# First norm on a third of the modulation, the rest of it made inside the RWKV rounds, and low-rank products on h and the difference

## The chip, the cores and the metric

The kernel runs on one core of one Trainium2 chip. The metric is the device time of one launch in microseconds: 3759.18 us is the median of three runs of the kernel before (3757.04 to 3760.25). TensorE (PE), VectorE (DVE), ScalarE (ACT), GpSimd (POOL) and SyncE (SP) run their own instruction streams, written out by hand, and hand over through semaphores. All DMAs are issued by SP, in program order.

## What is computed

The reference is a block of two layers (RWKV-7 time mix with MLP, then forgetting attention with MLP) and a second block (gated delta net, latent attention, mixture of experts), on 512 tokens of width 1024 in float32. The change touches only the first layer's modulation and time mix:

```python
c_act = silu(c)
mod = c_act @ mod_w[0] + mod_b[0]                 # 1024 -> 6144
sh1, sc1, gt1, sh2, sc2, gt2 = split(mod, 6)
h = rms_norm(x, norm_mix_g[0]) * (1 + sc1) + sh1
xx = token_shift(h) - h
xr, xw, xk, xv, xa, xg = (h + xx * mu[j] for j in range(6))
r, k, v = xr @ wr, xk @ wk, xv @ wv
w_log = -softplus(-(w0 + tanh(xw @ w1) @ w2)) - 0.5      # w1: 1024x64
a = sigmoid(a0 + (xa @ a1) @ a2)                          # a1: 1024x64
g = sigmoid(xg @ g1) @ g2                                 # g1: 1024x160
y = wkv7_scan(r, exp(-exp(w_log)), k, v, ...)             # in chunks of 64 tokens
x = x + (1 + gt1) * ((group_norm(y) + bonus) * g) @ wo
x = x + (1 + gt2) * mlp(rms_norm(x) * (1 + sc2) + sh2)
```

## The kernel before

Activations lie as 128 channels by 512 tokens in eight tiles (`x3`, `h3`). Weights pass through `W`, a ring of five slots of 128 x 2048 floats (1 MB). `load` takes the next slot, waits on SP until its former content is free (on DVE for kinds that begin with "md", on PE otherwise), and issues the DMAs. Because SP is one queue, a load that waits for its slot holds back every later one.

**Modulation.** The row of 6144 numbers is made in 12 groups of 512 columns, each from two 1 MB tiles. Of seven groups (0, 2, 4, 6, 7, 9, 11) DVE makes the sum over eight column blocks: one multiplication (L73) and seven multiply-adds (L76), accumulated in `rowb`; then four products of PE with a column of ones put the 512 sums into four columns of bank 6. The five groups in `MOD0_PE` are made by PE itself, with the activation of c as weights, and turned into columns in the same way over `rowp`. The function `dv_mod` waits for the last group, adds the bias and writes `mod0`, 48 columns: 0 to 7 shift, 8 to 15 scale, 16 to 23 gate, 24 to 47 those of the MLP. Only then does `dv_norm` form the gain and multiply x by the inverse root; ACT (`ac_normed`) scales and shifts tile by tile into `h3`.

**Mixing.** `dv_mix` makes the eight differences `xx3`. Then it forms the mixed inputs of w, a and g one tile at a time into two buffers in `MX`, each of which waits until PE has used the one two before; `pe_lora` multiplies each by w1, a1 or g1 (g1 in two parts of 96 and 64 columns, four banks in all). DVE then makes the mixed inputs of k and r, GpSimd (`gp_mix`) that of v. Before these loads `sp_mix` parks X in DRAM, since X is scratch in the rounds. The second low-rank weights (`lw2`) lie in slot 4 for the whole of the rounds, so the ring has four slots there.

**Rounds.** The 1024 channels are done in eight column blocks. Each passes five stages: `fetch` (k, r, v: 24 products of 128x128 by 512), `prep` (decay, normalised key), `scores` (chunk matrices and their inverse in five levels), `chain` (the state over eight chunks), `post` (group norm, gate, bonus). Round r runs chain on block r-3, scores on r-2, post on r-4, prep on r-1 and fetch on r. `woven` advances the stages by one step each in that order (3, 2, 4, 1, 0), on each engine by itself; a `yield` ends a step, and a stage has some 24 steps. So the position of an instruction in its engine's queue is set by its step and its stage, and a wait holds all that follows it on that engine. SP loads for round r two slots ("rk" with k and r, "rv" with v), and from round 4 a small one ("rg") with the gate's weights for `post`. After round 11, PE projects with `rw_wo` and DVE adds the result, scaled by one plus the gate, to the restored X.

Of the kernel before, what the change touches and what calls it, by code (L numbers as in the profile page):

```python
# [10 lines left out]
P = 128  # L11
T = 512
D = 1024
KT = 8
# [196 lines left out]
def program(nc, a, out):  # L211

    ctx = ExitStack()
    with ctx:
# [331 lines left out]

        cv = Carve()
# [5 lines left out]
        MX = cv(1024)  # L553
        omka = mods[:, 176:184]

        def sp_mix(sp):
            sp.wait_ge(s_ac, nac["nm", "mix0", 7])
            sp.dma(xpark, X[:, :]).then_inc(s_park, 16)
            load(sp, ("l1",), (0, (0, P), (8, 64), rows128(a["rw_w1"])), (512, (0, P), (8, 64), rows128(a["rw_a1"])),
                 (1024, (0, P), (8, 96), rows128(a["rw_g1"][:, 0:96])))  # L560
            load(sp, ("l2",), (0, (0, P), (8, 64), rows128(a["rw_g1"][:, 96:160])))
            ring.turn = NS - 1
            load(sp, ("lw2",), (0, (0, 64), (1024,), a["rw_w2"]), (0, (64, 128), (1024,), a["rw_a2"]),
                 (1024, (0, P), (640,), a["const"][:, NCON:NCON + 640]))
            ring.slots = NS - 1

        def dv_mix(dv):
            for k in range(KT):
                dv.wait_ge(s_ac, nac["nm", "mix0", k])
                dv.tt(xx3[:, k, 1:T], h3[:, k, 0:T - 1], h3[:, k, 1:T], SUB).then_inc(s_dv, ndv())  # L570
                dv.ts(xx3[:, k, 0:1], h3[:, k, 0:1], -1.0, None, MUL, None).then_inc(s_dv, ndv("xx", k))

            def mix(o, j, k):
                dv.wait_ge(s_dv, ndv["xx", k])
                return dv.stt(o, xx3[:, k, :], col("rw_mu", 8 * j + k), h3[:, k, :], MUL, ADD)

            n = 0
            for j in (1, 4, 5):
# [5 lines left out]
            for d, j in ((1, 2), (0, 0)):  # L584
                for k in range(KT):
                    mix(xm[d][:, k, :], j, k).then_inc(s_dv, ndv("xm", d, k))
            for k in range(KT):
                dv.wait_ge(s_gp, ngp["xm", k])
            dv.ts(omka, col("rw_ka", 0, 8), -1.0, 1.0, MUL, ADD).then_inc(s_dv, ndv("mixed"))

        def gp_mix(gp):
            for k in range(KT):
                gp.wait_ge(s_dv, ndv["xx", k])
                gp.ts(xm[2][:, k, :], xx3[:, k, :], col("rw_mu", 24 + k), None, MUL, None).then_inc(s_gp, ngp())
                gp.wait_ge(s_gp, ngp.n)
                gp.tt(xm[2][:, k, :], xm[2][:, k, :], h3[:, k, :], ADD).then_inc(s_gp, ngp("xm", k))

        def pe_lora(pe):
            k1, t1_ = ring["l1",]
            k2, t2_ = ring["l2",]  # L600
            w1v, a1v, g1v = [wv(k1, o, (0, P), (8, w)) for o, w in ((0, 64), (512, 64), (1024, 96))]
            g1w = wv(k2, 0, (0, P), (8, 64))
            n = 0
            for j in (1, 4, 5):
                for k in range(KT):
                    mb = MX[:, (n % 2) * 512:(n % 2) * 512 + 512]
                    f, l = k == 0, k == KT - 1
                    pe.wait_ge(ring.sems[k1], t1_)
                    pe.wait_ge(s_dv, ndv["mx", n])
                    if j == 1:  # L610
                        m = pe.mm(BK[0][0:64, :], w1v[:, k, :], mb, f, l)
                    elif j == 4:
                        m = pe.mm(BK[1][64:128, :], a1v[:, k, :], mb, f, l)
                    else:
                        pe.mm(BK[2][0:96, :], g1v[:, k, :], mb, f, l)
                        pe.wait_ge(ring.sems[k2], t2_)
                        m = pe.mm(BK[3][0:64, :], g1w[:, k, :], mb, f, l)
                    if n == 23:
                        npe.mark_next("free", "l1")
                        npe.mark_next("free", "l2")  # L620
                    m.then_inc(s_pe, npe("lora", n))
                    n += 1

        def ac_lora(ac):
            ac.wait_ge(s_pe, npe["lora", 7])
            ac.act(LO[0:64, :], BK[0][0:64, :], ACT.Tanh).then_inc(s_ac, nac("lo", 0))
            ac.wait_ge(s_pe, npe["lora", 15])
            ac.act(LO[64:128, :], BK[1][64:128, :], COPY).then_inc(s_ac, nac("lo", 1))
            ac.wait_ge(s_pe, npe["lora", 23])
            ac.act(ZG[0:96, 0:512], BK[2][0:96, :], ACT.Sigmoid).then_inc(s_ac, nac("lo", 2))  # L630
            ac.act(ZG[0:64, 512:1024], BK[3][0:64, :], ACT.Sigmoid).then_inc(s_ac, nac("lo", 3))
# [19 lines left out]
        XS, UU = cv(64), cv(64)  # L651
        yg = h3
# [30 lines left out]
        def pe_fetch(pe, ct, left):  # L683

            yield from idle(2)
            for j, name in enumerate(("k", "r", "v")):
# [6 lines left out]
                for k in range(KT):  # L693
                    if j == 2:
                        pe.wait_ge(s_gp, ngp["xm", k])
                    else:
                        pe.wait_ge(s_dv, ndv["xm", (1, 0)[j], k])
# [6 lines left out]
                    if k % 4 == 3:  # L704
                        yield from idle(3)

# [300 lines left out]
        def pe_chain(pe, ct):  # L1007
# [79 lines left out]
        def sp_post(sp, ct):  # L1087
            cs = slice(ct * 128, ct * 128 + 128)
            load(sp, ("rg", ct), (0, (0, 96), (128,), a["rw_g2"][0:96, cs]), (128, (0, 64), (128,), a["rw_g2"][96:160, cs]))

        def pe_post(pe, ct, left):
# [15 lines left out]
            pe.mm(BK[2][:, :], wv(kg, 0, (0, 96), (128,)), ZG[0:96, 0:512], True, False)  # L1107
            npe.mark_next("free", "rg", ct)
            pe.mm(BK[2][:, :], wv(kg, 128, (0, 64), (128,)), ZG[0:64, 512:1024], False, True).then_inc(s_pe, npe("g", ct))
# [47 lines left out]
        def sp_rwkv(sp):  # L1157
            sp_mix(sp)
            for r in range(12):
                if r < 8:  # L1160
                    sp_fetch(sp, r)
                if r >= 4:
# [6 lines left out]
        def pe_rwkv(pe):  # L1169
            pe_lora(pe)  # L1170
            left = {0: (s_ac, nac["lo", 0]), 1: (s_ac, nac["lo", 1]), 2: (s_ac, nac["lo", 2]), 3: (s_ac, nac["lo", 3])}
# [9 lines left out]
        def gp_rwkv(gp):  # L1181
# [3 lines left out]
            gp_mix(gp)  # L1185
            rounds(none, lambda c: gp_prep(gp, c), lambda c: gp_scores(gp, c), none, none)

        def dv_rwkv(dv):
# [3 lines left out]
            rounds(none, lambda c: dv_prep(dv, c), lambda c: dv_scores(dv, c), lambda c: dv_chain(dv, c), lambda c: dv_post(dv, c))  # L1192
# [1867 lines left out]
        def tensor_program(pe):  # L3060
            pe_start(pe)
            pe_squares(pe, "mix0", 7)
            run(pe_mod(pe, "mod0", 6144, 0, 6, MOD0_PE))
# [10 lines left out]
        def scalar_program(ac):  # L3074
# [5 lines left out]
            ac_mod(ac, "mod0", MOD0_PE)  # L3080
# [8 lines left out]
        def vector_program(dv):  # L3089
            dv_start(dv)  # L3090
            run(dv_mod(dv, "mod0", mod0, 6144, 0, col("mod_b0", 0, 48), 6, MOD0_PE))
# [112 lines left out]
```

## Time and profile before

| | |
|---|---|
| median of three runs | 3759.18 us (3757.04 to 3760.25) |
| the profiled execution | 3766.57 us, span 3764.8 us |
| mean granted clock of PE | 0.962 |
| busy, share of the span: PE / DVE / ACT / POOL | 94% / 38% / 19% / 11% |
| DMA | 452.62 MB, mean 120 GB/s |

A row of the timeline gives the start and the length of a merged group of instructions, the engine, the line, the operation, what it writes and reads, the count, and in brackets how long the engine stood idle before it and what ended that. Most matrix products of this kernel are recorded under line 79, a helper's, and most vector operations under L70, L73 and L76; they are told apart by tiles, shapes and order. In float32 one product of the program is two MATMUL instructions in the trace.

### The profile page before, as it was taken

The page shows a single profiled execution, that of the slowest core. Times are in us where ns is not written, and L with a number is a line of the kernel's source. Part 1 is how long each engine was busy: PE and PEld are TensorE (multiplying, and loading weights), DVE is VectorE, ACT ScalarE, POOL GpSimd, SP SyncE. Part 2 cuts the span into 40 slices and gives each one's busy share as a digit, 9 for nine tenths or more (in the row PEclk, how much of TensorE's full clock was granted, in tenths as well). Part 3 has the DMA queues.
Part 4 walks back from the last instruction along what each step waited for, and adds up shares of the span by engine and source line. Part 5 has one row for each costly group of instructions (what it writes and reads, how often), then busy time and mean ns, then how long its engine had stood idle before and what let it go on. Part 6 is the DMA issues. An engine that isn't in the chain of part 4 may idle for free.

```text
span 3764.8 us, 54477 instructions
## 1 busy us (share of the span) xinstructions
PE 3527.6 (94%) x24282; PEld 2173.7 (58%) x24282; DVE 1419.7 (38%) x2543; ACT 733.5 (19%) x1480; POOL 398.9 (11%) x310
## 2 busy tenths in 40 slices
PE   6699999899999999999998999998979999899998
PEld 2256667488884547588885566665434444434343
DVE  4543444288753005388633445453012211211011
ACT  1132333211003014211003222332012210200001
POOL 1210110123002000123001110102000001200000
PEclk8899998899999899999998999997989999999999
DMA  8310001255551120156522111000021114399996
GB/s 302 89 41 26 25 12 36 90 157 177 181 179 57 45 90 12 45 157 192 165 72 65 46 35 28 31 24 2 34 73 33 34 45 158 140 406 409 409 409 279
DMA packets 352746, 452.62 MB, mean 120 GB/s; under 512 B 18624, under 2 KB 258496, under 8 KB 352256
## 3 DMA queue, kind: packets, MB, share of 16 engines
q1 hardware_dynamic: 352512, 449.13, 34.8%
q8 instruction: 191, 3.13, 0.3%
q14 instruction: 43, 0.35, 0.0%
HBM read 444.87 MB, written 4.19 MB: 119 GB/s over the span
## 4 chain that ended last, share of the span: by engine, by line
PE 87%; DVE 5%; ACT 4%; DMA 2%; issue 1%; SPq 0%; POOL 0%; POOLq 0%; DVEq 0%; ACTq 0%
PE bank L79 87%; ACT A L87 2%; DVE A L76 1%; DVE A L70 1%; DMA A<-in_w_up 1%; ACT SM L87 1%; ACT H L87 0%; DMA W<-in_w_up 0%; ACT A L86 0%; DVE H L70 0%; SPq L93 0%; DVE X L76 0%; PE bank L82 0%; POOL SM L70 0%; DVE A L73 0%
## 5 line engine op out<-in xcount | busy, mean ns | idle before, releaser
L79 PE MATMUL bank<-A 64*64 64x64 f32 (+7 forms) x13408 | 1031.3, 261 | 62.2 <-ACT A L87 41.8
L79 PEld LDWEIGHTS bank<-A 64*64 64x64 f32 (+3 forms) x13408 | 813.6, 149 | 296.7 <-issue 134.6
L79 PE MATMUL bank<-A,W 128*128 128x512 f32 (+3 forms) x2336 | 829.6, 509 | 37.2 <-DMA W<-in_rw_g 18.4
L79 PE MATMUL bank<-H,W 128*128 128x512 f32 (+1 forms) x1776 | 694.5, 546 | 23.6 <-ACT H L87 11.4
L79 PEld LDWEIGHTS bank<-A,W 128*128 128x128 f32 (+2 forms) x2336 | 429.4, 189 | 383.7 <-issue 301.2
L79 PEld LDWEIGHTS bank<-H,W 128*128 128x128 f32 x1776 | 339.9, 195 | 343.0 <-issue 315.7
L87 ACT ACTIVATE A<-bank 128x512 f32<-128x512 f32 (+4 forms) x547 | 245.3, 451 | 1478.9 <-PE bank L79 1418.4
L70 DVE TENSOR_TENSOR A<-bank,A 128x256 f32<-128x256 f32 (+2 forms) x315 | 146.1, 476 | 402.3 <-PE bank L79 381.8
L79 PE MATMUL bank<-A,H 128*64 128x512 f32 (+1 forms) x1096 | 281.0, 595 | 11.7 <-ACT H L87 8.1
L70 POOL TENSOR_TENSOR A<-A 128x512 f32<-128x512 f32 (+1 forms) x111 | 155.6, 1407 | 1077.2 <-ACT A L87 372.1
L76 DVE SCALAR_TENSOR_TENSOR SM<-W,cact,SM 128x512 f32<-128x512 f32 x245 | 222.3, 907 | 11.8 <-DMA W<-in_mod_w 0.8
L79 PE MATMUL bank<-W,H 128*64 128x512 f32 (+3 forms) x952 | 212.3, 479 | 8.7 <-ACT H L87 5.5
L87 ACT ACTIVATE A<-A 128x512 f32<-128x512 f32 (+1 forms) x224 | 131.0, 609 | 448.8 <-DVE A L70 362.3
L79 PEld LDWEIGHTS bank<-A,H 128*64 128x64 f32 (+1 forms) x1096 | 89.9, 140 | 176.3 <-issue 149.5
L70 POOL TENSOR_TENSOR SM<-SM 128x512 f32<-128x512 f32 x40 | 52.3, 1307 | 1072.5 <-ACT SM L87 1070.5
L70 DVE TENSOR_TENSOR A<-bank,SM 128x512 f32<-128x512 f32 (+1 forms) x17 | 11.0, 686 | 403.2 <-PE bank L79 398.0
L76 DVE SCALAR_TENSOR_TENSOR X<-bank,mods,X 128x512 f32<-128x512 f32 (+1 forms) x120 | 81.3, 679 | 198.5 <-PE bank L79 195.1
L79 PEld LDWEIGHTS bank<-W,H 128*64 128x64 f32 (+1 forms) x952 | 87.4, 159 | 110.6 <-issue 99.9
L70 DVE TENSOR_TENSOR A<-W 128x512 f32<-128x512 f32 x128 | 91.9, 759 | 155.0 <-PE bank L79 87.5
L79 PE MATMUL bank<-A,con 128*128 128x512 f32 (+2 forms) x156 | 88.9, 658 | 20.5 <-ACT A L87 20.5
L87 ACT ACTIVATE H<-bank 128x512 f32<-128x512 f32 x56 | 31.8, 599 | 371.5 <-PE bank L79 348.1
L79 PE MATMUL bank<-H,A 128*128 128x256 f32 x384 | 93.3, 386 | 0.0
(164 smaller groups left out, 2412.5 us busy)
## 6 DMA issues: line engine op xcount, KB each, us to landing
W<-in_mod_w SPq DMA_DIRECT2D x48, 1024.0 KB, 7.2
A<-in_w_gate SPq DMA_DIRECT2D x47, 1024.0 KB, 18.5
A<-in_w_up SPq DMA_DIRECT2D x42, 1024.0 KB, 18.5
A<-in_w_down SPq DMA_DIRECT2D x40, 1024.0 KB, 18.7
W<-in_mlp_up SPq DMA_DIRECT2D x64, 512.0 KB, 5.3
W<-in_mlp_down SPq DMA_DIRECT2D x128, 256.0 KB, 3.9
W<-in_w_mod SPq DMA_DIRECT2D x24, 1024.0 KB, 5.2
W<-in_w_down SPq DMA_DIRECT2D x24, 1024.0 KB, 18.5
```

Of the source, the lines that this page charges most:

```text
L70: return self.e.tensor_tensor(o, x, y, op)
L76: return self.e.scalar_tensor_tensor(out=o, in0=x, scalar=s, in1=y, op0=op0, op1=op1, **kw)
L79: return self.e.matmul(o, l, r, start=start, stop=stop, skip_group_check=True)
L87: return self.e.activation(o, i, func, bias=bias, scale=scale)
```

## The change

Only modulation groups 0 to 3 are made before the norm: groups 0 and 2 on DVE, 1 and 3 on PE as before. Each of the other eight is made by DVE in one of rounds 0 to 7 (`dv_mod0`, stage fetch, one operation in each of steps 1, 4, 7, 10, 13, 16, 19 and 20), accumulated in `M0`, and turned into columns by PE (`pe_row0`): behind the fetch in rounds 0 to 2, ahead of the last chunk of the chain in rounds 3 to 7. Their bias is added after the rounds, in front of the gate. SP loads their two tiles in each round behind that round's k, r and v weights, through the same four slots.

The low-rank products use (h + xx mu) W = h W + xx (mu W). DVE multiplies the first low-rank weights by mu, row by row, into `LM`; PE multiplies h by the plain weights as the tiles of h appear, and then the differences by the scaled ones, into the same three banks. w1 and a1 lie side by side as one weight of 128 columns, g1 is taken as 128 and 32 columns, and the gate's second weights as 128 and 32 rows. Their loads go ahead of the parking of X and of the k, r and v weights. `gp_mix` goes, and DVE makes the mixed input of v too.

```diff
         def sp_mix(sp):
+            k, before = ring.take(("l1",), 3)
+            sp.wait_ge(...)
+            w1a1 = wv(k, 0, (0, P), (8, 128))
+            sp.dma(w1a1[:, :, 0:64], rows128(a["rw_w1"])).then_inc(ring.sems[k], 16)
+            sp.dma(w1a1[:, :, 64:128], rows128(a["rw_a1"])).then_inc(ring.sems[k], 16)
+            sp.dma(wv(k, 1024, (0, P), (8, 128)), rows128(a["rw_g1"][:, 0:128])).then_inc(ring.sems[k], 16)
+            load(sp, ("lw2",), ...)
+            load(sp, ("l2",), (0, (0, P), (8, 32), rows128(a["rw_g1"][:, 128:160])))
+            ring.slots, ring.turn = NS - 1, 1
+
+        def sp_park(sp):
             sp.wait_ge(s_ac, nac["nm", "mix0", 7])
             sp.dma(xpark, X[:, :]).then_inc(s_park, 16)
...
+            for i, (src, dst, j, c) in enumerate(((0, 0, 1, slice(0, 64)), (0, 0, 4, slice(64, 128)), (1, 1, 5, slice(0, 128)), (2, 2, 5, slice(0, 32)))):
+                n = c.stop - c.start
+                mu = col("rw_mu", 8 * j, 8).unsqueeze(2).broadcast_to([P, 8, n])
+                dv.tt(low_mu[dst][:, :, c], w[src][:, :, c], mu, MUL).then_inc(s_dv, ndv("lm", i))
+            for d, j in ((1, 2), (0, 0), (2, 3)):
                 for k in range(KT):
-                    if n >= 2:
-                        dv.wait_ge(s_pe, npe["lora", n - 2])
-                    mix(MX[:, (n % 2) * 512:(n % 2) * 512 + 512], j, k).then_inc(s_dv, ndv("mx", n))
-                    n += 1
...
+                    dv.wait_ge(s_dv, ndv["xx", k])
+                    dv.stt(xm[d][:, k, :], xx3[:, k, :], col("rw_mu", 8 * j + k), h3[:, k, :], MUL, ADD).then_inc(s_dv, ndv("xm", d, k))
...
+        def pe_lora(pe):
...
+            outs = BK[0][:, :], BK[1][:, :], BK[2][0:32, :]
+            for part in range(2):
                 for k in range(KT):
+                    if part:
+                        pe.wait_ge(s_dv, ndv["lm", 3])
                     else:
+                        pe.wait_ge(s_ac, nac["nm", "mix0", k])
+                    for o, w in zip(outs, lowrank(low_mu if part else low_loaded(), k)):
+                        m = pe.mm(o, w, (xx3 if part else h3)[:, k, :], part == 0 and k == 0, part == 1 and k == 7)
...
+        def sp_mod0(sp, r):
+            for hf in range(2):
+                load(sp, ("md", "mod0", 4 + r, hf), (0, (0, P), (4, 512), rows128(a["mod_w0"][hf * 512:(hf + 1) * 512, (4 + r) * 512:(5 + r) * 512])))
+
+        def dv_mod0(dv, r):
+            g, acc = 4 + r, M0[r % 2]
+            for hf in range(2):
+                k, there = ring["md", "mod0", g, hf]
+                v = wv(k, 0, (0, P), (4, 512))
+                for j in range(4):
+                    yield
+                    if j == 0:
+                        dv.wait_ge(ring.sems[k], there)
+                    c = cact[:, 4 * hf + j:4 * hf + j + 1]
+                    if hf == 0 and j == 0:
...
+                        m = dv.ts(acc, v[:, j, :], c, None, MUL, None)
+                    else:
+                        dv.wait_ge(s_dv, ndv["m0", r, 4 * hf + j - 1])
+                        m = dv.stt(acc, v[:, j, :], c, acc, MUL, ADD)
+                    if j == 3:
+                        ndv.mark_next("free", "md", "mod0", g, hf)
+                    m.then_inc(s_dv, ndv("m0", r, 4 * hf + j))
+                    if 4 * hf + j < 6:
+                        yield
+                        yield
...
+        def pe_row0(pe, r):
+            pe.wait_ge(s_dv, ndv["m0", r, 7])
+            for j in range(4):
+                c = 256 + 4 * r + j
+                m = pe.mm(BK[6][:, c:c + 1], M0[r % 2][:, j * 128:(j + 1) * 128], C("ones", 1), True, True)
+            m.then_inc(s_pe, npe("row0", r))
...
         # pe_fetch, at its end
+            if ct < 3:
+                pe_row0(pe, ct)
+            yield from idle(4)
...
         # pe_chain
                     pe.wait_ge(s_dv, ndv["sp", ct, c])
+                    if c == 7 and ct + 3 < 8:
+                        pe_row0(pe, ct + 3)
...
         # dv_rwkv
+            dv.wait_ge(s_pe, npe["row0", 7])
+            dv.tt(mod0[:, 16:48], BK[6][:, 256:288], col("mod_b0", 16, 32), ADD).then_inc(s_dv, ndv("mod", "mod0"))
...
-        MOD0_PE = (1, 3, 5, 8, 10)
+        MOD0_PE = (1, 3)
...
-            run(sp_mod(sp, "mod0", a["mod_w0"], 6144, MOD0_PE))
+            run(sp_mod(sp, "mod0a", a["mod_w0"], 2048, MOD0_PE))
+            sp_mix(sp)
             sp_rwkv(sp)
```

## Rows read from the trace of the kernel before

**Rows 1.** The page: chain that ended last, by engine; one DMA issue group
```profile
PE 87%; DVE 5%; ACT 4%; DMA 2%; issue 1%; SPq 0%; POOL 0%; POOLq 0%; DVEq 0%; ACTq 0%
...
W<-in_mod_w SPq DMA_DIRECT2D x48, 1024.0 KB, 7.2
```

**Rows 2.** Timeline, 0 to 110 us: modulation groups 3 and 11, one DVE group, the norm
```profile
45.38 9.88 PE L79 MATMUL bank<-W,cact 128*1 128x512 f32 x16
...
55.93 1.05 PE L79 MATMUL bank<-con,A 1*128 1x1 f32 x8 [0.68 <-ACT A L87]
...
61.16 5.54 DVE L76 SCALAR_TENSOR_TENSOR SM<-W,cact,SM 128x512 f32<-128x512 f32 x7
...
99.08 1.05 PE L79 MATMUL bank<-con,SM 128*128 128x1 f32 x8
...
101.42 5.75 ACT L87 ACTIVATE H<-H,mods 128x512 f32<-128x512 f32 x8 [3.37 <-DVE H L70]
```

**Rows 3.** SP's issues at 42 us, and low-rank weights: size, time to landing
```profile
42.29 1.47 SPq L93 DMA_DIRECT2D W<-in_mod_w  x3
...
W<-in_rw_g SPq DMA_DIRECT2D x1, 384.0 KB, 9.2
```

**Rows 4.** Timeline, 142 to 193 us: low-rank products, ScalarE behind them, first fetch
```profile
142.12 0.24 PEld L79 LDWEIGHTS bank<-A,W 128*96 128x96 f32 x2 [0.81 <-issue]
...
144.15 0.24 PEld L79 LDWEIGHTS bank<-A,W 128*96 128x96 f32 x2 [0.81 <-issue]
...
154.41 1.07 ACT L87 ACTIVATE A<-bank 96x512 f32<-96x512 f32 x2 [14.42 <-PE bank L79]
...
164.74 28.46 PE L79 MATMUL bank<-A,W 128*128 128x512 f32 x60 [10.36 <-DMA W<-in_rw_wr]
```

**Rows 5.** Stretches: busy time (and count) per engine, PE's granted clock, DMA share, GB/s
```profile
57.90:61.70 3.80, 3.80 (x6) 0.59 (x6) 1.02 (x2) 0.00 (x0) 0.00 (x0) 0.55 1.04 401
138.00:154.40 16.40, 16.38 (x33) 3.48 (x32) 8.55 (x13) 1.88 (x2) 0.00 (x0) 1.00 0.00 0
164.70:170.70 6.00, 5.96 (x7) 2.52 (x8) 0.00 (x0) 0.00 (x0) 0.00 (x0) 0.51 1.05 257
437.70:441.00 3.30, 3.30 (x38) 3.13 (x37) 0.78 (x2) 1.32 (x3) 0.00 (x0) 0.61 0.20 50
```

**Rows 6.** SP's issue that waited for the first v weights to be used
```profile
188.53 0.37 SPq L93 DMA_DIRECT2D W<-in_rw_wv  x1
```

**Rows 7.** Timeline of DVE and PE at the ends of rounds 2 and 3
```profile
260.59 0.68 DVE L70 TENSOR_TENSOR H<-bank,SM 128x512 f32<-128x512 f32 x1
...
260.73 0.33 PE L79 MATMUL bank<-A 64*64 64x64 f32 x4 [0.79 <-DVE A L1000]
...
313.96 0.68 DVE L70 TENSOR_TENSOR H<-bank,SM 128x512 f32<-128x512 f32 x1
314.56 0.27 DVE L76 SCALAR_TENSOR_TENSOR A<-A,bank 128x64 f32<-128x64 f32 x1
...
314.88 0.45 PE L79 MATMUL bank<-A 64*64 64x64 f32 x8 [0.34 <-DVE A L76]
```

**Rows 8.** PE's r product and gate product in a round; the gate weights' landing
```profile
349.47 3.70 PE L79 MATMUL bank<-A,W 128*128 128x512 f32 x8
...
355.35 2.18 PE L79 MATMUL bank<-A,W 96*128 96x512 f32 x4
...
W<-in_rw_g SPq DMA_DIRECT2D x1, 32.0 KB, 2.0
```

**Rows 9.** Timeline of PE: score products at the start of rounds 5 and 6
```profile
377.07 1.92 PE L79 MATMUL bank<-A,X 64*64 64x128 f32 x32
...
437.68 3.18 PE L79 MATMUL bank<-A,X 64*64 64x128 f32 x32
```

**Rows 10.** Middle of round 3: DVE's masked copy of a level, PE's products that read it
```profile
300.56 0.68 DVE L70 TENSOR_TENSOR A<-bank,W 128x512 f32<-128x512 f32 x1
...
303.56 3.95 PE L79 MATMUL bank<-A 64*64 64x64 f32 x128
```

More of the change, by code:

```diff
@@ L598, in pe_lora @@
[L598 to L613, printed above, removed]
-                    else:
[L615 to L622, printed above, removed]
@@ new lines, in dv_mix @@
+            for key in ("l1", "l2"):
+                k, there = ring[key,]
+                dv.wait_ge(ring.sems[k], there)
+            w = low_loaded()
+            for i, (src, dst, j, c) in enumerate(((0, 0, 1, slice(0, 64)), (0, 0, 4, slice(64, 128)), (1, 1, 5, slice(0, 128)), (2, 2, 5, slice(0, 32)))):
+                n = c.stop - c.start
+                mu = col("rw_mu", 8 * j, 8).unsqueeze(2).broadcast_to([P, 8, n])
+                dv.tt(low_mu[dst][:, :, c], w[src][:, :, c], mu, MUL).then_inc(s_dv, ndv("lm", i))
@@ new lines, in dv_mix @@
+            for d, j in ((1, 2), (0, 0), (2, 3)):
+                for k in range(KT):
+                    dv.wait_ge(s_dv, ndv["xx", k])
+                    dv.stt(xm[d][:, k, :], xx3[:, k, :], col("rw_mu", 8 * j + k), h3[:, k, :], MUL, ADD).then_inc(s_dv, ndv("xm", d, k))
+            dv.ts(omka, col("rw_ka", 0, 8), -1.0, 1.0, MUL, ADD).then_inc(s_dv, ndv("mixed"))
+        def pe_lora(pe):
+            for key in ("l1", "l2"):
+                k, there = ring[key,]
+                pe.wait_ge(ring.sems[k], there)
+            outs = BK[0][:, :], BK[1][:, :], BK[2][0:32, :]
+            for part in range(2):
+                for k in range(KT):
+                    if part:
+                        pe.wait_ge(s_dv, ndv["lm", 3])
+                    else:
+                        pe.wait_ge(s_ac, nac["nm", "mix0", k])
+                    for o, w in zip(outs, lowrank(low_mu if part else low_loaded(), k)):
+                        m = pe.mm(o, w, (xx3 if part else h3)[:, k, :], part == 0 and k == 0, part == 1 and k == 7)
+                if part:
+                    npe.mark_next("free", "l1")
+                    npe.mark_next("free", "l2")
+                m.then_inc(s_pe, npe("lora", part))
@@ new lines, in ac_lora @@
+            ac.act(ZG[:, 0:512], BK[1][:, :], ACT.Sigmoid).then_inc(s_ac, nac("lo", 2))
+            ac.act(ZG[0:32, 512:1024], BK[2][0:32, :], ACT.Sigmoid).then_inc(s_ac, nac("lo", 3))
+        def sp_mod0(sp, r):
[9 more added lines that the diff above has]
+                    if j == 0:
+                        dv.wait_ge(ring.sems[k], there)
+                    c = cact[:, 4 * hf + j:4 * hf + j + 1]
+                    if hf == 0 and j == 0:
+                        if r >= 2:
+                            dv.wait_ge(s_pe, npe["row0", r - 2])
+                        else:
+                            dv.wait_ge(s_dv, ndv["mixed"])
+                        m = dv.ts(acc, v[:, j, :], c, None, MUL, None)
+                    else:
+                        dv.wait_ge(s_dv, ndv["m0", r, 4 * hf + j - 1])
[6 more added lines that the diff above has]
+                        yield
+            yield
+            yield
+            yield
+            yield
@@ L651, in program @@
         XS, UU = cv(64), cv(64)
+        M0 = [cv(512) for _ in range(2)]
         yg = h3
@@ L3062, in tensor_program @@
             pe_squares(pe, "mix0", 7)
[L3063 removed]
+            run(pe_mod(pe, "mod0a", 2048, 0, 6, MOD0_PE))
             pe_rwkv(pe)
@@ L3079, in scalar_program @@
             ac_rstd(ac, "mix0", 7)
-            ac_mod(ac, "mod0", MOD0_PE)
+            ac_mod(ac, "mod0a", MOD0_PE)
             ac_rwkv(ac)
```

65 lines of the change are left out of this document (23 added, 42 removed).

## The prediction

> **What bounds the kernel now.** I read the page first. Its chain of the work that ended last is 87% on PE [rows 1], and PE is busy for 94% of the span, so an edit pays where PE stands still or does work that need not stand in the path. Then I read the start in order of time. The first normalised tile waits for all 24 modulation tiles. Modulation group 3 is finished on PE at 55.93 + 1.05 = 56.98 us, group 11 at 99.08 + 1.05 = 100.13 us [rows 2]; ScalarE begins the first normalised tile 1.29 us after that and needs 0.72 us for it (5.75 us for eight) [rows 2]. Everything between 56.98 and 100.13 serves columns 16 to 47 of `mod0`, which the norm does not read. After the norm comes a stretch in which the low-rank products hold PE until 154.4 us, and PE then has nothing until 164.74 us, because the projection weights stand behind them in the DMA queue [rows 4]. The first of eight fetch stages (k, r, v) gives its last weight slot back at 188.53 us [rows 6]. From there to about 640 us PE is nearly full, with short waits at the end of every round. What is added there lengthens the program; the question of this case is how much of the start's gain the rounds give back.
>
> **The change, step by step.** *Modulation.* Groups 0 to 3 keep their engines and order, so row 3 ends at 56.98 us as before: 43.15 us earlier than row 11 does now. The first tile of h is there at 56.98 + 1.29 + 0.72 = 59.0 us. The low-rank weights now follow the eighth modulation tile on SP; the slot they need is given back at 42.29 us, where the trace shows three issues in 1.47 us [rows 3]. Seven issues end by about 47 us. Their landing is bounded by that of the same weights before, 9.2 us beside the 2 MB parking transfer [rows 3]: 56 us. So they are hidden by the modulation itself, with 3 us to spare; without that cover each late microsecond would be paid in full. Parking and the first projection weights come after the last h tile (59.0 + 5.0 = 64 us), and have 45 us before anyone needs them, so the gap of 10 us before the first fetch goes.
>
> *Low-rank products.* Before, 32 products of 128x512 waited on mixed inputs; now there are 48 (three outputs, eight tiles, once on h, once on the difference), each two instructions. At half clock seven instructions took 6.0 us [rows 5], 0.857 each, so 0.43 at full clock: 96 x 0.43 = 41.2 us. They need nothing from VectorE but the eight differences (about 7 us) and four multiplications for the scaled weights (3 us, estimated by size from 0.69 us for 512 columns [rows 7]): done near 73 us, while the first half of the products alone runs to beyond 80. The 24 mixes for k, r, v are then 24 x 0.7 = 17 us on VectorE, done near 90 us, again behind PE. GpSimd's share of the mixing goes and nothing takes its place. The trace shows that four instructions alternating between 96 and 64 output columns take 144.15 − 142.12 = 2.03 us [rows 4] at granted clock 1.00 [rows 5], against 4 x 0.43 = 1.71: 0.16 us for each alternation. The new order is 128, 128, 32 columns, two alternations per tile, 32 in all: 5.1 us. Bounds: 0 (if it doesn't recur) and 0.32 each, 10 us; I take 0.16, the only row that has it.
> The Trainium skill, page "TensorEngine Tiling (Array Packing)", Key Properties, says that changing the tiling mode drains the engine. That speaks against a 32-column product between 128-column ones, and it would make 5.1 us of the 46.3; by instruction count alone the time would come out at 3727 us.
> PE restarts at 59.0 after two idle microseconds; at 57.90 us, after a similar pause, it ran for 3.8 us at granted clock 0.55 [rows 5], at the fetch for 6.0 us at 0.51. That loses half, 1.9 to 3.0 us; I take 2.5. End of the products: 59.0 + 2.5 + 41.2 + 5.1 = 107.8 us.
> ScalarE then makes tanh and a copy before bank 0 is free, two steps like the pair that took 1.07 us [rows 4], so 1.3 us with the hand-over: the first fetch starts at 109.1 instead of 164.74. It took 188.5 − 164.7 = 23.8 us, of which 3.0 were the half clock's loss [rows 5]; PE pauses for only 1.3 us now, so I drop these: end at 129.9 instead of 188.5. **Gain up to here: 58.6 us.**
>
> *Rounds.* VectorE makes one group per round, eight operations of 5.54 / 7 = 0.79 us [rows 2], 6.3 us a round, 50 us in all. In the middle of a round this is hidden: the level's masked copy is made by 301.2 us and PE reads it at 303.56 [rows 10], which leaves 2.3 us for one added operation of 0.79, and VectorE idles before the other copies. At a round's end it is not. The seventh and eighth operations stand at weave steps 19 and 20, around the state update which PE waits for. In round 3 the sequence is: output product at 313.96, ready for a successor at 314.6, state update at 314.56, PE starts 0.34 us late at 314.88 [rows 7]. With the two operations: 314.6 + 0.8, update 0.2, + 0.8 = 316.4, and then PE makes row r before it goes on. A row is 8 instructions of one column, 1.0 us (1.05 with its end [rows 2]). So 316.45 + 1.0 − 314.88 = 2.6 us for each of rounds 3 to 7: 13.0 us. In round 2 the row stands behind the last fetch: the product ends at 261.2, the operations at 262.8, the row at 263.9, where PE went on at 260.73 [rows 7]: 3.2 us. In rounds 0 and 1 VectorE is done in time, 1.0 us each. Sum 18.2 us.
> The ring now holds one round ahead instead of two. The next round's first modulation tile is issued at the end of the round and lands within 7.2 us (median of 48) [rows 1]; VectorE wants it some 4 us into the round, after its masks and the two biases, and in round 1 and 2 it will be 2 to 3 us late. There VectorE was idle for the decay anyway, and I price this at 1.0 us in all (0 to 6).
> From round 4 the gate weights go into the slot that the same round's k and r weights held. These are free at 353.2, after the r product [rows 8]; two issues of 0.4 us (three took 1.47 [rows 3]) and 2.0 us to land [rows 8] make 356.0 us, and PE wanted them at 355.35 [rows 8]: 0.7 us, in rounds 4 to 7: 2.8 us (0 to 8).
> *The clock.* After a tail of small products and waits one round, at 437.68 us, began at granted clock 0.61 [rows 5], and its first 32 score instructions took 3.18 us; after an equal tail at 377.07 they took 1.92 us [rows 9]. The balance is fine, and the tails of rounds 2 to 7 now have 2.6 us more in which PE does nearly nothing. One such start costs 3.18 − 1.92 plus 0.4 ahead of it, 1.7 us, and up to 3.0 if it lasts as at the fetch. I take 2.0 for each of the five round starts that ran at full clock: 10 us (0 to 15).
> The Trainium skill, page "TensorE: Matmul & The Clock Gate", section "HAM oscillation", warns that pauses of PE send it back to half rate; by that rule all five are paid, without it the time would be 3722 us. Which one holds this trace doesn't settle, since it has both kinds of tail.
> *Behind the rounds* VectorE adds one small addition before the gate; the first residual waits for a projection of 10 us, which hides it. The output weights are taken in other slots and land earlier; before, too, they were not waited for.
>
> **Sum.** 58.6 − 18.2 − 1.0 − 2.8 − 10 = 26.6 us. The profiled execution was 3766.57 us (span 3764.8 and 1.8 around it), which becomes 3740; it ran 7.4 us above the median of 3759.18, so on the scale of the medians I forecast **3732 us**.
>
> **Rivals.** (1) *The clock holds* and the tails overlap better: 58.6 − 14 or less, 3708 to 3718 us. For it: of the two round starts in [rows 9] one stayed at full clock, though behind a shorter tail than these will be. Chance 0.17. (2) *VectorE falls behind in the rounds*: its added 6.3 us a round does not fit between PE's hand-overs, or GpSimd's traffic stretches the 0.79 us; if each round loses 2 us more than counted, 16 us: 3748. Against it are the idle stretches before nearly every VectorE operation. Chance 0.14. (3) *The change ends slower*: the modulation tile blocks VectorE's queue at the start of each round. All masks, scans and state updates stand behind that wait, and PE behind them. It decides once a tile is later than VectorE's slack by more than 26.6 / 7 = 3.8 us in each of seven rounds; if a tile needed 7.2 us after the start of the round and each of the two tiles were waited for once, 7 x 7 = 49 us are lost, less the 1.0 counted: 3780 us. Against it: the issue comes at least 3 us before the round starts. Chance 0.05. (4) *The start gains less*: the low-rank weights land after 59 us, because their rows are short (128 to 512 bytes) and three kinds stand ahead of them, or the alternations cost 0.32; 5 to 10 us lost: 3740. Chance 0.12. The forecast itself, from 3720 to 3740: 0.52.
>
> **How the numbers follow.** The likeliest case gives 3732. The range leaves out rival 3 and the best half of rival 1: 3711 to 3750. A measurement of this kernel tells 0.2%, 7.5 us, from no change. Slower takes rival 3, 0.05; the same takes the edge of rival 2, 0.04; faster the rest, 0.91.
>
> **What would show it.** The row of group 3 ends near 57 us, PE's low-rank products start near 59 and end near 108, and the first fetch starts near 109; four instructions of 128 columns take 1.7 us and a tile's six 2.9. Each of rounds 3 to 7 should be 2.6 us longer before any change of clock, with eight one-column instructions in its tail, and its start should show a clock under 1. The gate product of rounds 4 to 7 should wait less than 1 us for its weights. I am wrong if the low-rank products wait for weights or VectorE, if the middle of a round shows new waits of PE on VectorE, or if the rounds together grow by less than 15 or by more than 50 us.

## The result, and the profile after

The changed kernel took 3726.11 us (median of six runs, 3723.16 to 3736.06) against 3759.72 for the kernel before in the same comparison; the ratio is 0.992, with a 95% interval of 0.9896 to 0.9944. I measured it twice more beside the experiments: 3727.89 against 3754.39 (ratio 0.9928, 0.9913 to 0.9943) and 3731.38 against 3756.48 (0.9929, 0.9908 to 0.9951). So the gain is 25 to 34 us, and the two later comparisons, with eleven runs of the kernel before each, say 25 to 27. The forecast was 3732 us and a gain of 26.6.

The page hardly changes, since PE bounds both (busy time of the engines and the chain; for before see the table and [rows 1]):

```profile
PE 3504.2 (94%) x24266; PEld 2169.1 (58%) x24266; DVE 1422.2 (38%) x2556; ACT 730.7 (20%) x1477; POOL 376.9 (10%) x294
...
PE 87%; DVE 5%; ACT 4%; DMA 2%; issue 1%; POOL 0%; SPq 0%; POOLq 0%; DVEq 0%; ACTq 0%
```

The start, from the timeline of the changed kernel (start, length, engine, operation, count, idle before):

```profile
54.45 1.05 PE L79 MATMUL bank<-con,A 1*128 1x1 f32 x8 [0.68 <-ACT A L87]
...
57.71 24.76 PE L79 MATMUL bank<-H,W 128*128 128x512 f32 x48 [2.21 <-ACT H L87]
...
68.82 15.98 DVE L76 SCALAR_TENSOR_TENSOR A<-A,cols,H 128x512 f32<-128x512 f32 x24
82.41 23.19 PE L79 MATMUL bank<-A 128*128 128x512 f32 x48
...
106.94 20.84 PE L79 MATMUL bank<-A,W 128*128 128x512 f32 x48 [1.34 <-issue]
```

Group 3 ends at 55.5 us, where [rows 2] had 56.98 for it; the products run without a gap from 57.71 to 105.6 us, the fetch follows after 1.34 us and ends at 127.8, where [rows 6] has 188.5. VectorE is done with its 24 mixes at 84.8 us, 22 us before anyone needs them.

The end of round 3, VectorE and PE (compare [rows 7] and [rows 9]):

```profile
260.06 0.74 DVE L76 SCALAR_TENSOR_TENSOR A<-W,cact,A 128x512 f32<-128x512 f32 x1
260.72 0.27 DVE L76 SCALAR_TENSOR_TENSOR A<-A,bank 128x64 f32<-128x64 f32 x1
260.91 0.74 DVE L76 SCALAR_TENSOR_TENSOR A<-W,cact,A 128x512 f32<-128x512 f32 x1
...
261.80 1.02 PE L79 MATMUL bank<-con,A 128*128 128x1 f32 x8 [1.75 <-DVE A L76]
...
265.08 3.00 PE L79 MATMUL bank<-A,X 64*64 64x128 f32 x32
```

The state update (260.72) stands between the two added operations, and PE waits 1.75 us for the second one before it makes the row; before, it waited 0.34 us. Then the next round starts at a lower clock: granted clock 0.62 from 265 to 268 us, and 3.00 us for the 32 score instructions instead of 1.92. In round 2, which has no chain yet, the row stands behind the last fetch:

```profile
203.62 1.05 PE L79 MATMUL bank<-con,A 128*128 128x1 f32 x8 [2.84 <-DVE A L76]
```

The lead over the kernel before, taken where the score products of a round start on PE (rounds are counted from 0, the first scores stand in round 2), shows how the rounds give the start's gain back:

| start of the scores in round | 2 | 3 | 4 | 6 | 7 | 9 | output projection |
|---|---|---|---|---|---|---|---|
| before, us | 212.01 | 260.90 | 316.83 | 437.68 | 499.18 | 600.63 | 680.15 |
| changed, us | 152.86 | 204.77 | 265.08 | 394.77 | 463.12 | 569.73 | 640.99 |
| lead, us | 59.2 | 56.1 | 51.8 | 42.9 | 36.1 | 30.9 | 39.2 |

The lead falls from 60.7 us at the first fetch's end to 30.9 where the last of the added work is behind. From there on PE runs the same instructions in both kernels (only the rows of the gate product are split otherwise, and its four instructions take 2.18 us in both), and the lead nevertheless grows to 39.2 us at the output projection and to 42.9 at the end of the span (3764.8 against 3721.9 us). The experiments show what that is.

### The profile page after: what moved, and what is told of

The parts are those of the page before. It is cut to its first block, busy times and chain, and to the rows that moved or that the text cites. A ratio compares the mean times of both kernels' runs of the same rounds, so it can differ in the third digit from the quotient of the medians.

```text
span 3721.9 us, 54427 instructions
## 1 busy us (share of the span) xinstructions
PE 3504.2 (94%) x24266; PEld 2169.1 (58%) x24266; DVE 1422.2 (38%) x2556; ACT 730.7 (20%) x1477; POOL 376.9 (10%) x294
## 4 chain that ended last, share of the span: by engine, by line
PE 87%; DVE 5%; ACT 4%; DMA 2%; issue 1%; POOL 0%; SPq 0%; POOLq 0%; DVEq 0%; ACTq 0%
PE bank L79 87%; ACT A L87 2%; DVE A L76 1%; DVE A L70 1%; DMA A<-in_w_up 1%; ACT SM L87 1%; ACT H L87 1%; DMA W<-in_w_up 0%; DVE H L70 0%; ACT A L86 0%; DVE X L76 0%; DVE SM L76 0%; POOL SM L70 0%; DVE A L73 0%; DMA A<-in_x 0%
## 5 line engine op out<-in xcount | busy, mean ns | idle before, releaser
L79 PE MATMUL bank<-A 64*64 64x64 f32 (+7 forms) x13456 | 1051.4, 261 | 62.0 <-ACT A L87 42.0
L79 PE MATMUL bank<-A,W 128*128 128x512 f32 (+2 forms) x2272 | 792.5, 504 | 9.5 <-DVE A L76 3.6
L79 PE MATMUL bank<-H,W 128*128 128x512 f32 (+3 forms) x1824 | 718.8, 548 | 26.9 <-ACT H L87 14.1
L79 PEld LDWEIGHTS bank<-A,W 128*128 128x128 f32 (+1 forms) x2272 | 420.6, 189 | 327.1 <-issue 287.4
L79 PEld LDWEIGHTS bank<-H,W 128*128 128x128 f32 (+2 forms) x1824 | 344.5, 193 | 365.1 <-issue 334.0
L87 ACT ACTIVATE A<-bank 128x512 f32<-128x512 f32 (+6 forms) x544 | 243.2, 450 | 1454.5 <-PE bank L79 1444.6
L76 DVE SCALAR_TENSOR_TENSOR SM<-W,cact,SM 128x512 f32<-128x512 f32 x210 | 193.1, 920 | 9.5
L76 DVE SCALAR_TENSOR_TENSOR X<-bank,mods,X 128x512 f32<-128x512 f32 (+1 forms) x120 | 81.2, 679 | 197.5 <-PE bank L79 194.1
## 6 DMA issues: line engine op xcount, KB each, us to landing
W<-in_w_down SPq DMA_DIRECT2D x24, 1024.0 KB, 18.4
```

What stands on the lines that cost most here:

```text
L76: return self.e.scalar_tensor_tensor(out=o, in0=x, scalar=s, in1=y, op0=op0, op1=op1, **kw)
L79: return self.e.matmul(o, l, r, start=start, stop=stop, skip_group_check=True)
L87: return self.e.activation(o, i, func, bias=bias, scale=scale)
```

## The experiments

**The reference runs.** The changed kernel, unaltered, beside the first and beside the second group of experiments.

> The changed kernel unaltered, as the reference for the runs beside it. Its trace showed the start 60.7 us ahead at the first fetch's end and 39.2 us ahead at the output projection, 42.9 us at the end of the span. Expected: 30 to 43 us faster than the kernel before. If the 3.7 us gained behind the rounds are only where PE's clock happened to fall, another execution need not show them.

> The changed kernel again, as the reference of this call. Expected within 0.3% of its other runs, 30 to 43 us faster than before.

Measured: 26.5 and 25.1 us faster than before, by the medians. From the start of the scores in round 9 to the output projection (rounds 9 to 11, the same instructions in all these kernels) the traces show 79.5 us before, 71.3 in the first profile of the changed kernel, 71.9 and 77.7 in these two; from the projection to the end 3084.7 us before and 3080.9, 3083.9 and 3084.8. So the 12 us of lead gained behind round 9 belong to the two executions that were profiled and not to the change: that of before was 10.7 us above the median of fifteen runs (3755.85), and one and the same changed kernel took 71.3 to 77.7 us for the first of the two stretches. Both expectations of 30 to 43 us were missed, 26.5 and 25.1, since they were read from that one pair of executions.

**No modulation in the rounds.** Leaves the eight later groups out.

```diff
-                    sp_mod0(sp, r)
...
-            rounds(lambda c: dv_mod0(dv, c), lambda c: dv_prep(dv, c), ...
+            rounds(none, lambda c: dv_prep(dv, c), ...
...
-            dv.tt(mod0[:, 16:48], BK[6][:, 256:288], col("mod_b0", 16, 32), ADD)
+            dv.e.tensor_copy(mod0[:, 16:48], col("mod_b0", 16, 32))
```

> Leaves out the eight later modulation groups altogether (no loads, no VectorE operations, no rows; columns 16 to 47 of the modulation are the bias alone), so it prices what the rounds pay for them. My theory (the tails pay: 1.0 us a row, 1.4 us of wait in each of five tails, 2 us in round 2, and a lower clock at six round starts): about 16 to 19 us less than the changed kernel, near 3706 us, with the middles of the rounds unaltered. Rival (VectorE is late in the middle of rounds too): more than 25 us less. Rival (the tails are hidden and only the rows cost): 8 us less.

Measured: 3694.2 us, 33.7 less than the changed kernel beside it. My 16 to 19 us were wrong, and by the number it is the rival that VectorE is late in mid-round; the trace says otherwise. From the start of the scores in round 3 to that in round 4 it takes 55.9 us against 60.5 in the changed kernel. Of that difference of 4.5, 1.76 − 0.34 + 1.02 = 2.4 stand in the tail, since the old wait of 0.34 stays; the other 2.1 are left for the lower clock around it. PE's waits for the chain's VectorE operations (L76) in the rounds are 2.0 us here and 12.0 there, where six of the seven are the waits ahead of a row:

```profile
PE bank L79 <- DVE A L76: 2.0, 6, 0.3
```

```profile
PE bank L79 <- DVE A L76: 12.0, 7, 2.8
```

(the waits from 130 to 620 us, this kernel first, then the changed one: total, times, longest). The comparison also has a flaw of mine: with fewer loads the ring ends at another slot, and the output weights are issued only at 611.07 us, when the last gate product has given its slot back:

```profile
616.57 57.39 PE L79 MATMUL bank<-H,W 128*128 128x512 f32 x128 [5.53 <-DMA W<-in_rw_wo]
```

5.53 instead of 1.42 us, so the rounds without the work are 4.1 us better than they look. From the first fetch to the projection it is 507.1 against 534.2 us; with the 4.1 the work in the rounds costs 31.2 us. The forecast of the change had 32.0 for it (rows and waits 18.2, modulation tiles 1.0, gate weights 2.8, clock 10). Where the flaw can't reach, from the first fetch to the scores of round 9, it is 432.9 against 462.3 us, 29.4 less. Of these, eight rows at full clock are 8.1, the waits for L76 10.0 less one of 0.8 us for another operation that only this kernel shows, and the gate weights 1.4; the remaining 10.7 us are left for the clock. That is the term that my 16 to 19 us left out: rows and waits alone fill them. The medians differ by more than the rounds do. In the two traces 10.7 us of the difference lie behind the start of the projection (3073.2 against 3083.9 us), where the edit changes no instruction of PE, and that part stays unexplained.

**Operations early in the round.** In pairs at steps 5, 8, 11 and 14.

```diff
-                    yield
+                    if j % 2 == 0:
+                        yield from idle(5 if hf == 0 and j == 0 else 3)
...
-                    if 4 * hf + j < 6:
-                        yield
-                        yield
-            yield
-            yield
-            yield
-            yield
+            yield from idle(10)
```

> One part altered: the eight VectorE operations of a round stand in pairs at steps 5, 8, 11 and 14, right behind the masked copy of a level, and none at steps 19 and 20; rows where they were. Tail theory: the wait of 1.76 us ahead of each row in rounds 3 to 7 falls to the old 0.34, the one of 2.84 us in round 2 to 0.8: 9 us. Clock theory: with the shorter tails the round starts return to full clock, another 5 to 10 us; so 14 to 19 us in all. If the clock falls for other reasons: 9 us and starts still at 0.6 to 0.8. If the middle of a round has no room for two operations at once, the gain is below 5 us and new waits of PE on VectorE appear there.

Measured: 3716.42 us (ratio to before 0.9898, 0.9879 to 0.9916), 11.5 less than the changed kernel beside it. Its end of round 3:

```profile
257.33 1.05 PE L79 MATMUL bank<-con,A 128*128 128x1 f32 x8 [0.34 <-DVE A L76]
...
260.26 1.92 PE L79 MATMUL bank<-A,X 64*64 64x128 f32 x32
```

The wait is the old 0.34 us, and the start runs at full clock, as do those of rounds 3, 5 and 6; rounds 7 and 8 still took 3.62 and 3.09 us. The tail theory holds: the waits for L76 are 2.0 us in total, 10.0 less than in the changed kernel, and the longest is 0.34. So the middles had room too. The clock theory holds in the trace and not in the median. From the first fetch to the scores of round 9 it takes 445.6 us instead of 462.3, 16.7 less, of which 10.0 are the waits and 6.7 are left for the clock; but the stretch from there to the projection, with the same instructions, took 77.2 instead of 71.9 (granted clock 0.86 from 560 to 620 us, 1.00 in the changed kernel). The six runs lie 18 us apart, the profiled one is the fastest, and their median falls short of the expected 14. How much of the clock part lasts to the end they don't settle.

**Fillers in the wait.**

```diff
+            for _ in range(5 if r > 2 else 8 if r == 2 else 0):
+                pe.mm(BK[6][:, 288:512], C("ones"), con[:, 0:224], True, True)
             pe.wait_ge(s_dv, ndv["m0", r, 7])
```

> PE makes extra products of constants into unused columns of bank 6 ahead of each row wait (eight in round 2, five in rounds 3 to 7, 1.9 to 3.0 us at full clock), results unused. This separates the clock from the wait: the wait stays, PE is busy in it. Clock theory: the starts of rounds 3 to 8 run at full clock, so 6 to 10 us less than the changed kernel. Rival (the clock falls whatever PE does in the tail): no gain, or 0 to 3 us slower.

Measured: 3726.26 us, 1.6 less than the changed kernel and within what the runs scatter, so the expected 6 to 10 us did not come. The trace separates what the time does not:

```profile
261.20 2.16 PE L79 MATMUL bank<-con 128*128 128x224 f32 x10 [1.00 <-DVE A L76]
...
266.02 1.92 PE L79 MATMUL bank<-A,X 64*64 64x128 f32 x32
```

With PE busy in the wait the starts of rounds 3 to 8 all took 1.92 us, where the changed kernel's took 2.7 to 3.5, and the granted clock from 200 to 560 us was 1.00 instead of 0.96. That shows that the lower clock of these six starts follows from PE's idleness in the tail. It is not all that counts: round 9, whose tail has neither a row nor fillers, now took 3.36 us, where the changed kernel's took 1.92. And the fillers can begin only after the state update, 1.00 us into the wait, and the row then starts 3.80 us after the group of 20 products ahead of it instead of 2.56: 1.2 us late in each of five rounds, 6 us in all, which eats most of what they save. From the first fetch to the projection it takes 530.3 us instead of 534.2, with two waits for gate weights (1.68 and 1.48 us) where the changed kernel had one of 1.41.

**The old products on the new order.** Modulation and loads as changed, low-rank products, their mixing and the gate's split as before.

```diff
-                        for o, w in zip(outs, lowrank(low_mu if part else low_loaded(), k)):
-                            m = pe.mm(o, w, (xx3 if part else h3)[:, k, :], ...)
+                    pe.wait_ge(s_dv, ndv["mx", n])
+                    ...
+                        m = pe.mm(BK[0][0:64, :], w1v[:, k, :], mb, f, l)
```

> Keeps the changed modulation and the early loading of the low-rank and projection weights, but makes the low-rank products as before: mixed inputs by VectorE and GpSimd, 32 products paced by two buffers. Theory A (the products' new form is what shortens the stretch from norm to fetch): fetch starts 10 us or more later than with the new form. Theory B (the new form trades a start 12 us sooner for 16 more products and their alternations, and the stretch was shortened by the loads alone): the old form takes about 49 us from the modulation's end to the fetch against 51.4, so the two kernels are within 3 us of each other. I hold B.

Measured: 3727.11 us, against 3731.38 of the changed kernel beside it and 3727.89 beside the first experiments, so no difference clear of the scatter. In the trace PE waits longer and then has less to do:

```profile
69.34 9.59 PE L79 MATMUL bank<-A,W 128*64 128x512 f32 x14 [14.28 <-DVE A L76]
```

From the addition of the bias that ends the modulation (55.10 us) to the scores of round 2 (152.46) it takes 97.4 us, with the new products 98.3 (56.53 to 154.86). Theory B holds: the algebra is worth about nothing in time.

**The narrow products together.** 128-column products of all eight tiles first, then the eight of 32 columns.

```diff
             for part in range(2):
-                for k in range(KT):
...
+                for wide in (True, False):
+                    for k in range(KT):
```

> One part altered: the eight products of 32 columns of each half are made behind the sixteen of 128 columns instead of between them: 4 alternations instead of 32. Drain theory (0.16 us for each change of width): the second half of 24 products takes 20.8 us instead of 23.2, in all 4 to 5 us less than the changed kernel. Rival (a product of 32 columns is itself slower): no change in the stretch.

Second half of the products, the changed kernel (after_same) and this one:

```profile
84.41 23.19 PE L79 MATMUL bank<-A 128*128 128x512 f32 x48
```

```profile
82.59 20.98 PE L79 MATMUL bank<-A 128*128 128x512 f32 x48
```

2.21 us for fourteen alternations fewer, 0.16 each, where the rival, a product of 32 columns that is itself slower, forecast no change: the cost goes with the changes of width. The Trainium skill, page "TensorEngine Tiling (Array Packing)", Key Properties, says that changing the tiling mode drains the engine; these two rows agree with it, though no row shows the drain itself. The fetch starts at 104.92 instead of 108.94 us. Of these 4.0 us the trace has 0.6 left at the scores of round 5 (the starts of rounds 3, 4 and 5 took 3.62 us each instead of 2.99, 2.72 and 3.30), 3.0 at those of round 9, and 0.4 at the projection (642.69 against 643.11). The other execution of the changed kernel gives 0.9, 3.0 and 6.2 at the same places. The median of 3726.53 is 4.9 us below the changed kernel beside it and 1.4 below its other reference, so the time can't tell the expected 4 to 5 us from none.

**The two halves of the change alone.** First the kernel before with only the loads of the low-rank weights put ahead of the parking:

```diff
         def sp_mix(sp):
-            sp.wait_ge(s_ac, nac["nm", "mix0", 7])
-            sp.dma(xpark, X[:, :]).then_inc(s_park, 16)
+            ring.turn = NS * 5
             load(sp, ("l1",), ...)
             load(sp, ("l2",), ...)
-            ring.turn = NS - 1
+            ring.turn = NS * 6 - 1
             load(sp, ("lw2",), ...)
-            ring.slots = NS - 1
+            ring.slots, ring.turn = NS - 1, 2
+            sp.wait_ge(s_ac, nac["nm", "mix0", 7])
+            sp.dma(xpark, X[:, :]).then_inc(s_park, 16)
```

> The kernel before with one part of the change: the low-rank weights and the second low-rank weights are loaded ahead of the parking of X, each in a slot of its own, so the projection weights no longer stand behind the last product. Modulation, products and rounds as before. By the trace of before it should save the wait of the first product (118.5 instead of about 113.4: 5 us), the gap ahead of the fetch (10.4 less 0.7: 10 us) and the half clock at the fetch's start (3 us): 18 us, 3736 to 3740 us. If instead the loads were hidden anyway, within 5 us of before.

Then the changed modulation with the old load order and the old products:

```diff
         def sp_park(sp):
             sp.wait_ge(s_ac, nac["nm", "mix0", 7])
             sp.dma(xpark, X[:, :]).then_inc(s_park, 16)
+            ring.turn = 2 * NS - 1
+            load(sp, ("l1",), ...)
+            load(sp, ("l2",), ...)
+            ring.turn = NS - 1
+            load(sp, ("lw2",), ...)
+            ring.slots = NS - 1
```

> The changed kernel's modulation (four groups ahead of the norm, eight in the rounds), with the loads behind the parking of X as before and the low-rank products as before. Start: 43 us sooner. Rounds: they pay what leaving the work out gave back, 27 to 31 us. So 12 to 16 us faster than before, 3740 to 3744 us; with the 18 us of the loads that adds up to the 27 to 30 us of the whole change. A rival is that the two halves don't add: beyond 25 us here would mean that the loads bring little by themselves.

Measured: 3742.87 us (0.9964, 0.9951 to 0.9977) and 3742.43 us (0.9962, 0.9949 to 0.9976), against 3755.85: 13.0 and 13.4 us, in sum 26.4, and the whole change measured 26.5. Each half is uncertain by about 5 us, so that the sum comes so close is luck; what holds is that neither half is the whole. The loads alone give 17.2 us of lead at the scores of round 2 (194.82 against 212.01) and 18.4 at the projection (661.78 against 680.15), as expected, though only 13.0 by the medians, which misses 3736 to 3740 us: the 18 us were read against an execution of before 10.7 us above its median, and the profiled execution here was 5.6 above its own. In the other kernel both waits of the old order are there, the second one as in [rows 4]:

```profile
74.22 7.51 PE L79 MATMUL bank<-A,W 128*64 128x512 f32 x10 [18.35 <-DMA W<-in_rw_g]
...
120.85 19.32 PE L79 MATMUL bank<-A,W 128*128 128x512 f32 x40 [10.03 <-DMA W<-in_rw_wr]
```

It has the flaw of the kernel without modulation as well: its output weights stand in another slot and are waited for 5.16 us instead of 1.42. By the difference of these two waits this half would be some 3.7 us larger without it.

**Three repairs together**, and then a fourth. The first two are the edits shown above; of the third, the buffer `G2` and its loads are shown, which SP also issues ahead of the round's other loads.

```diff
+        G2 = [cv(256) for _ in range(2)]
...
-            load(sp, ("rg", ct), ...)
+            sp.dma(g[:, 0:128], a["rw_g2"][0:128, cs]).then_inc(ring.sems[k], 16)
+            sp.dma(g[0:32, 128:256], a["rw_g2"][128:160, cs]).then_inc(ring.sems[k], 16)
```

> Three parts together: the modulation operations early in the round, the 32-column products grouped, and the gate weights in a buffer of their own, so that their loads wait for no slot of the round. By the sum of the parts (9 us of waits, 4.5 us of alternations, 1.5 to 3 us of gate weights, 5 to 10 us of clock) 20 to 26 us faster than the changed kernel, 3700 to 3706 us; without the clock part 15 us.

Measured: 3709.0 us (0.9874, 0.9851 to 0.9896), 22 us less than the changed kernel beside it and 19 less than its other reference, so above the expected 3700 to 3706 us, with a gain at the lower edge of 20 to 26. Nothing waits for gate weights any more, but the starts of rounds 4, 5, 7 and 8 were slow (3.62, 3.09, 3.62 and 2.96 us).

```diff
-                    if c == 7 and ct + 3 < 8:
+                    if c == 6 and ct + 3 < 8:
                         pe_row0(pe, ct + 3)
```

> The fastest kernel so far with one part altered: in rounds 3 to 7 the row is made ahead of the seventh chunk of the chain instead of the eighth, before the tail in which PE waits, so that the tail is 1.0 us shorter. The row itself costs PE the same. Clock theory: of four slow round starts two return to full clock, 2 to 5 us less. Rival (which tails fall into the lower clock is a matter of when they come, not of their length by a microsecond): within 2 us of it.

```profile
251.35 0.95 PE L79 MATMUL bank<-con,A 128*128 128x1 f32 x8
...
257.13 1.92 PE L79 MATMUL bank<-A,X 64*64 64x128 f32 x32
```

Measured: 3703.71 us (0.9855, 0.9836 to 0.9873), the fastest, 52 us under the kernel before. Of the round starts 3 to 9 one was slow (round 5, 3.19 us). The step from 3709.0 is 5.3 us, measured apart and with overlapping intervals, so the time alone doesn't prove it. The rows agree with the clock theory: three of the four slow starts returned, and from the first fetch to the scores of round 9 it takes 438.6 us instead of 446.6. But 4.4 of these 8.0 us are lost again on the way to the projection (78.4 against 74.0 us for the same instructions).

## Why the prediction was right, point by point

*Modulation and norm.* Right. The end of group 3 was put at 56.98 us and came at 55.5 to 56.6 in the three traces of the changed kernel, the first product at 57.7 to 58.8 instead of 59.0. The cover of the low-rank weights held: no wait for them.

*Low-rank products.* Right in size: 48.8 us forecast with half clock and alternations, 47.9 and 48.9 measured (57.71 to 105.6, 58.70 to 107.6). The 0.16 us an alternation, taken from products of 96 and 64 columns, held for 128 and 32. What the forecast had not said is that the old products would have done as well: I priced the new form without pricing the old one on the same start. The gain that was carried as one number, 58.6 us (60.7 and 58.7 measured), is the modulation and the load order alone.

*The fetch at full clock.* Right: 20.84 us, granted clock 1.00.

```profile
106.90:128.00 21.10, 21.06 (x53) 9.61 (x53) 5.75 (x8) 4.97 (x7) 0.00 (x0) 1.00 0.46 149
```

*Rows and waits.* Right. Rounds 3 to 7 were given 2.6 us each, and the trace has 1.75 − 0.34 + 1.0 = 2.4. Round 2 was given 3.2 and took 2.84 − 0.79 + 1.0 = 3.05. By the kernel without modulation in the rounds all rows and waits come to 8.1 + 10.0 − 0.8 = 17.3 us, against 18.2 in the sum.

*Loads.* Sized wrong in both terms, by little. Modulation tiles were late to VectorE twice (6.5 us in all) and at no cost to PE, where the sum had 1.0. The gate weights were forecast late by 0.7 us in each of four rounds, 2.8 in all. Three rounds show no wait of PE for them and one shows 1.48, more than the "less than 1 us" of the forecast: the smaller of the two loads (16 KB) landed 3.3 us after its issue, where the forecast had taken 2.0. Behind that wait the clock fell too, which the sum did not have:

```profile
435.93 2.19 PE L79 MATMUL bank<-A,W 128*128 128x512 f32 x4 [1.48 <-DMA W<-in_rw_g]
```

The 32 products of two 64x64 tiles that start at 438.32 us took 1.92 us, where the same ones take 1.10 in the other rounds.

*The clock.* Right in kind and size, 10 us forecast and 10.7 left for it by the kernel without modulation. The forecast took five more slow starts at 2 us. The trace has six slow starts (2.59, 3.00, 3.52, 3.00, 2.97 and 3.44 us), five more than before up to there. The other two traces of the changed kernel have six as well, in the same rounds. Rival 1, that the clock holds, fell: in the changed kernel it did not, and the fillers show why. The forecast leaned on the Trainium skill, page "TensorE: Matmul & The Clock Gate", section "HAM oscillation", for "all five are paid". The rows agree with its warning that a pause costs the clock, but the pauses that it describes are waits for DMA longer than any of these (2.84 us at most), so that these short tails are enough is shown by the runs and not by that section. Over the rounds the forecast gave back 32.0 us; the lead fell by 60.7 − 30.9 = 29.8.

*Rivals 2 and 3*, VectorE late in mid-round or blocked by a tile: no new wait of PE on VectorE in the middle of a round. *Rival 4*, a late start: no.

*The sum* stood against one execution of before, 3766.57 us, and was carried over to the median as a difference. That was needed: the pair of profiled executions differs by 42.9 us, the medians by 25 to 34. The profiled excess was put at 7.4 us from three runs, and over fifteen it is 10.7. The range, 3711 to 3750, took in no term for it. That 26.6 meets 25 to 27 so closely is partly luck: where the added work ends, the three traces have leads of 29.4 to 30.9 us, 3 to 4 more than the sum, of which the loads explain 2 to 3, and behind that place the clock takes and gives several microseconds that no term had.

## What to carry to other kernels

Work taken out of the head of a program and spread into a saturated loop costs what it adds at the places where the bounding engine waits already: here 31 of 59 us came back. Part of that was only eight short operations at the wrong steps: moving these to where their engine idled in any case gave 11.5 us back, and with three small repairs more the gain doubled. Before crediting a rewrite of the arithmetic, run its other half alone: reordering a few loads brought about half the gain, and the new algebra none. And compare leads at landmarks of the trace, since behind the change the same instructions differed by up to 12 us from one execution to the next.

## What the runs showed of the hardware

PE's granted clock at the start of a round followed what PE had done in the tail ahead of it (wait, row and small products against fillers, row and small products), and seemingly also when the tail came: with 4.0 us saved ahead of the rounds and nothing else altered, three starts went from 2.99, 2.72 and 3.30 to 3.62 us each, and the saving shrank to 0.6 us and came back to 3.0. Two executions of the changed kernel 0.1 us apart at the scores of round 2 agree in their six slow starts to 0.13 us, and the third, 2.0 us sooner there, differs from them by up to 0.4. That speaks for the moment and against chance, but no run varied the moment alone. From the output projection to the end the same instructions took between 3073 and 3085 us in the traces of this case. A row of eight one-column products took 1.02 us at the end of round 3 and 1.84 at the end of round 5, where the lower clock was already granted:

```profile
390.29 1.84 PE L79 MATMUL bank<-con,A 128*128 128x1 f32 x8 [1.76 <-DVE A L76]
```

So a saving of a few microseconds in a kernel like this can't be read from one execution, nor a loss of as much.
